# Narrow expert jobs of a mixture layer in plain float32, two 64-column stationary tiles side by side

## The chip, the core and the metric

One core of a Trainium2 chip. The metric is the device time of one execution in microseconds, the median of several runs. Engines: TensorE (PE, with its weight loads PEld), VectorE (DVE), ScalarE (ACT), GpSimd (POOL) and SyncE (SP), which here only issues DMAs.

## What is computed

A two-layer decoder step for 320 tokens (256 of a prompt, 8 x 8 of samples), width 1024. Layer 0 has a dense channel mixer, layer 1 a mixture of eight experts with the two best per token:

```python
def _swiglu(h, w_gate, w_up, w_down):
    return (jax.nn.silu(h @ w_gate) * (h @ w_up)) @ w_down

def _moe(h, w_router, b_router, w_gate, w_up, w_down):
    logits = (h @ w_router).astype(jnp.float32) + b_router.astype(jnp.float32)
    top_vals, top_idx = lax.top_k(logits, TOP_K)
    wts = jax.nn.softmax(top_vals, axis=-1)
    combine = jnp.sum(jax.nn.one_hot(top_idx, N_EXPERTS, dtype=jnp.float32) * wts[..., None], axis=-2)
    out = jnp.zeros_like(h)
    for e in range(N_EXPERTS):
        out = out + combine[..., e:e + 1] * _swiglu(h, w_gate[e], w_up[e], w_down[e])
    return out
```

w_gate and w_up are 1024 x 2816 per expert, w_down 2816 x 1024, all float32: 34.6 MB per expert.

## The kernel before

Everything up to 1207 us of the profile (both token mixers, the dense mixer, the router) is left as it is. Then the experts are worked off as jobs. A job takes up to 128 tokens (wide) or up to 64 (narrow) of one expert and streams all of that expert's weights. Jobs 0, 2, 4 and 6 are wide, jobs 1, 3, 5, 7 narrow; experts with more tokens get further narrow jobs at the end, up to six (`EXTRA`); with these inputs there is one, job 8. So nine jobs run, nine times 34.6 MB.

A job has 35 pairs of DMAs. Pairs 0 to 23 are gate and up columns in three column groups of eight pairs (one pair for each 128 rows of the 1024): 512 columns twice for gate and twice for up in groups 0 and 1 (1 MB per pair), 384 in group 2 (0.79 MB). Pairs 24 to 34 are two 128-row blocks of w_down each (1 MB). SyncE loads a pair n into slot n % 7 of the ring MRAW (L536) once pair n - 7 is used up (semaphore `m_used`). The first pair of a group is used up only with the second, since its second half of columns waits for a PSUM bank.

Weights are split into a rounded high part and a low part in the format fp32r, a matmul format that TensorE takes at one column per cycle: ScalarE copies a pair to MHI (`m_hi_part`, L1774, a ring of five), VectorE subtracts and writes MLO over the raw pair (`m_lo_part`, L1170). Both engines run ahead of TensorE by a fixed number of pairs in their program order, across the ends of jobs.

Wide job: tokens are split into XEH and XEL too, and each weight tile takes three matmuls (L2590 high x high, L2592 low x high, L2597 high x low; for w_down L2630, L2632, L2637 with the gated values GTH and GTL). Narrow job: the 64 tokens' high parts and their low parts stand side by side as 128 stationary columns, so two matmuls per weight tile (L2590, L2597; L2630, L2637) do it, and the two halves of the result are folded when it is turned: four PSUM tiles are copied by ScalarE (SG L1819, SU L1824), 88 small matmul calls pass them with FOLD (L2652) to the transposed layout, ScalarE and VectorE form silu(gate) x up and split it anew (L1849, L1414, L1807, L1368).

Between pairs, side work stands in a table by hand (`SIDE`): eight `combine` units in pairs 2 to 9 (L2549, L2550: the scaled output of the job before, YEH and YEL, through the placement matrix PTS into SA by VectorE L1409), six `turn` units (pairs 10, 11, 18, 19, 26, 27), `place` at 13, `pick` at 16, which frees POOL to gather the next job's tokens (L1989, 128 rows of 4 KB), and the two `fill` transposes at 28 and 30 that make the next job's stationary operand.

At a job's end ScalarE copies the output, scaled by the routing weight SW, to YEH (L1835) and VectorE makes YEL (L1390, `y_made`). TensorE's pair 1 of the next job waits for `y_made` before it takes the banks of the second column half. Each engine waits on its queue in order. After the last job SyncE loads three filler pairs (L562) that the ahead-running splits still count on. VectorE then releases the index semaphore for the gathers of the jobs that are not there (L1447), and POOL makes them one after another.

Pairs and landings below are counted per job from 0.

Of the kernel before, what the change touches and what calls it, by code (L numbers as in the profile page):

```python
# [99 lines left out]
TURN_OF = {tile_at(k)[0]: k for k in range(TURNS)}  # L100
TURN_PAIRS = {p: [k for _, what, k in units if what == "turn"] for p, units in SIDE.items()}
# [138 lines left out]
def build(nc, a, out):  # L240
    ctx = ExitStack()
    with ctx:
# [121 lines left out]
        SU = at("su", [P, 2, 512], F32, O_H1 + 18432)  # L364
        SGT = at("sgt", [P, 2, 4 * HALF], F32, O_H1 + 22528)
        FOLD = at("fold", [P, HALF], F32, O_H1 + 32768)
# [68 lines left out]
        half_lo = sem("half_lo")  # L435
# [36 lines left out]
        def _(sp):  # L472
# [80 lines left out]
            extra = sp.value_load(XI[0:1, 15:16], min_val=1, max_val=1 + EXTRA)  # L553
# [18 lines left out]
        def _(dve):  # L572
# [593 lines left out]
            def m_lo_part(job, n):  # L1166

                w = 4 * GROUPS[n % PAIRS // KD][1] if n % PAIRS < GPAIRS else 2 * D
                dve.wait_ge(m_hi, job * PAIRS + (n + 1))
                V.tensor_tensor(MLO[:, n % RAW_RING, 0:w], MRAW[:, n % RAW_RING, 0:w],  # L1170
                                MHI[:, n % HI_RING, 0:w].bitcast(F32), ALU.subtract).then_inc(m_lo, 1)
# [14 lines left out]
            def low_fill(k, number, half):  # L1186

                dve.wait_ge(xe_hi, number + 1)
                src, s = PS[:, FILL_BANKS[k], :].rearrange("p (k n) -> p k n", k=4), slice(4 * k, 4 * k + 4)
                if half:  # L1190
                    V.tensor_tensor(XEH[:, s, HALF:P], src[:, :, HALF:P], XEH[:, s, 0:HALF].bitcast(F32),
                                    ALU.subtract).then_inc(xe_out, 1)
                else:
                    V.tensor_tensor(XEL[:, s, :], src, XEH[:, s, :].bitcast(F32), ALU.subtract).then_inc(xe_out, 1)
# [56 lines left out]
            for k in range(2):  # L1251
                low_fill(k, k, False)
# [1476 lines left out]
```

## Time and profile before

| what | us |
|---|---|
| median of three runs (2090.72 to 2104.79) | 2097.79 |
| the profiled execution | 2101.74 |
| its span, first to last instruction | 2099.9 |
| TensorE busy, matmuls | 1964.0 |
| VectorE busy | 1427.4 |
| ScalarE busy | 1142.0 |
| mean granted clock of TensorE, share of 2.4 GHz | 0.977 |

The span is cut into stretches at the ends of jobs. A view of busy time by stretch gives for each engine the busy time and the number of instructions, then the granted clock, the DMA share and the rate. A timeline gives start, duration, engine, line, operation and tiles, and in brackets how long the engine sat idle before it and what released it. Matmuls are pipelined: the distance of two starts is what one costs, not its duration. A plain float32 matmul stands in the trace as two MATMUL instructions with two weight loads.

### The profile page before, as it was taken

To read this page: it belongs to the slowest core of one execution; us is meant where nothing else is said; L and a number is where in the kernel's file an instruction comes from. 1 tells how busy PE (TensorE), PEld (TensorE's weight loads), DVE (VectorE), ACT (ScalarE), POOL (GpSimd) and SP (SyncE) were. 2 spreads that over 40 slices of the span, in tenths; PEclk is the share of its full clock that TensorE was granted. 3 is DMA by queue.
4 is the path that set the end of the run, shared out by engine and by line. 5 is a ranking of instruction groups with operands and counts; after the bars stand their busy time and mean duration, and the time that the engine had idled before them with its cause. 6 is when DMAs were issued, how large, how long until landed. Compare 5 with 4: busy or idle time off the path is not lost. (4 is left out here: it accounts for less than half of the span.)

```text
span 2099.9 us, 34064 instructions
## 1 busy us (share of the span) xinstructions
PE 1964.0 (94%) x13043; PEld 1749.7 (83%) x13043; DVE 1427.4 (68%) x1617; ACT 1142.0 (54%) x1207; POOL 135.8 (6%) x172
## 2 busy tenths in 40 slices
PE   7999999999999999999999899989999988998894
PEld 5999999988999889989989788868777877887673
DVE  4476545555444455845455599998989898988985
ACT  4434334344443343423344477786778677777874
POOL 3100003200000030000140100000000000000000
PEclk8999999999999999999999999999999999999997
DMA  9635465564666454335565479999999999999995
GB/s 346 211 98 156 131 196 176 192 200 130 211 202 217 145 153 153 110 92 171 172 200 191 177 283 384 354 403 332 380 360 384 345 367 389 335 403 352 409 357 194
DMA packets 244412, 528.27 MB, mean 252 GB/s; under 512 B 18183, under 2 KB 142201, under 8 KB 244258
## 3 DMA queue, kind: packets, MB, share of 16 engines
q1 hardware_dynamic: 234304, 495.78, 66.2%
q0 software_dynamic: 9936, 30.34, 4.6%
q8 instruction: 105, 1.72, 0.3%
q14 instruction: 49, 0.40, 0.1%
q10 hardware_dynamic: 18, 0.04, 0.0%
HBM read 513.49 MB, written 12.59 MB: 251 GB/s over the span
## 5 line engine op out<-in xcount | busy, mean ns | idle before, releaser
L1170 DVE TENSOR_TENSOR mlo<-mraw,mhi 128x2048 fp32r<-128x2048 f32 (+1 forms) x317 | 680.2, 2167 | 24.3 <-ACT mhi L1774 22.4
L1774 ACT ACTIVATE mhi<-mraw 128x2048 fp32r<-128x2048 f32 (+1 forms) x318 | 576.9, 1822 | 205.2 <-DMA mraw<-in_w_exp_up 96.0
L584 DVE TENSOR_TENSOR wlo<-raw,whi 128x1024 fp32r<-128x1024 f32 x244 | 289.1, 1213 | 315.4 <-ACT whi L1483 314.3
L2092 PE MATMUL ps<-h1h,whi 128*128 128x320 f32 x1248 | 388.6, 323 | 6.6 <-DVE h1l L691 3.9
L2093 PE MATMUL ps<-h1l,whi 128*128 128x320 f32 x1248 | 373.6, 311 | 0.0
L1483 ACT ACTIVATE whi<-raw 128x1024 fp32r<-128x1024 f32 x244 | 247.7, 1046 | 116.7 <-PE ps L2477 44.8
L2590 PE MATMUL ps<-mhi,xeh 128*128 128x512 f32 (+1 forms) x864 | 281.1, 388 | 16.7 <-issue 6.7
L2092 PEld LDWEIGHTS ps<-h1h,whi 128*128 128x128 f32 x1248 | 237.8, 191 | 23.1 <-issue 17.8
L2093 PEld LDWEIGHTS ps<-h1l,whi 128*128 128x128 f32 x1248 | 237.9, 191 | 0.2 <-issue 0.2
L2597 PE MATMUL ps<-mlo,xeh 128*128 128x512 f32 (+1 forms) x864 | 230.3, 378 | 0.0
L2138 PE MATMUL ps<-h1h,wlo 128*128 128x320 f32 x1248 | 210.1, 311 | 0.0
L2590 PEld LDWEIGHTS ps<-mhi,xeh 128*128 128x128 f32 x864 | 160.6, 193 | 41.4 <-issue 9.9
L2138 PEld LDWEIGHTS ps<-h1h,wlo 128*128 128x128 f32 x1248 | 190.0, 189 | 0.4 <-issue 0.4
L2597 PEld LDWEIGHTS ps<-mlo,xeh 128*128 128x128 f32 x864 | 162.4, 192 | 25.5 <-DVE mlo L1170 0.9
L2592 PE MATMUL ps<-mhi,xel 128*128 128x512 f32 (+1 forms) x384 | 143.6, 374 | 0.0
L2630 PE MATMUL ps<-mhi,gth 128*128 128x512 f32 x396 | 131.5, 400 | 0.0
L2637 PE MATMUL ps<-mlo,gth 128*128 128x512 f32 x396 | 111.1, 402 | 20.8 <-DVE mlo L1170 20.3
L2637 PEld LDWEIGHTS ps<-mlo,gth 128*128 128x128 f32 x396 | 71.3, 188 | 50.1 <-DVE mlo L1170 36.7
L2630 PEld LDWEIGHTS ps<-mhi,gth 128*128 128x128 f32 x396 | 72.8, 188 | 13.8
L2592 PEld LDWEIGHTS ps<-mhi,xel 128*128 128x128 f32 x384 | 72.6, 189 | 8.8
L2092 PE MATMUL ps<-h2h,whi 128*128 128x320 f32 x256 | 77.0, 315 | 0.0
L1989 POOL DMA_INDIRECT xg<-h_rows,idx x15 | 18.1, 1204 | 897.0 <-DVE idx L1430 814.6
(445 smaller groups left out, 2792.1 us busy)
## 6 DMA issues: line engine op xcount, KB each, us to landing
mraw<-in_w_exp_down SPq DMA_DIRECT2D x198, 512.0 KB, 9.3
mraw<-in_w_exp_gate SPq DMA_DIRECT2D x150, 512.0 KB, 6.2
mraw<-in_w_exp_up SPq DMA_DIRECT2D x144, 512.0 KB, 7.6
raw<-in_w_in SPq DMA_DIRECT2D x128, 512.0 KB, 3.8
raw<-in_w_ada SPq DMA_DIRECT2D x64, 512.0 KB, 3.8
mraw<-in_w_exp_gate SPq DMA_DIRECT2D x72, 384.0 KB, 3.8
mraw<-in_w_exp_up SPq DMA_DIRECT2D x72, 384.0 KB, 5.0
pause<-in_w_ada SPq DMA_DIRECT2D x32, 512.0 KB, 7.2
```

The source lines that it names most:

```text
L584: V.tensor_tensor(WLO[:, u % RAW_UNITS, 0:w], RAW[:, u % RAW_UNITS, 0:w], WHI[:, h % HI_UNITS, 0:w].bitcast(F32), ALU.subtract).then_inc(l ...
L1170: V.tensor_tensor(MLO[:, n % RAW_RING, 0:w], MRAW[:, n % RAW_RING, 0:w], MHI[:, n % HI_RING, 0:w].bitcast(F32), ALU.subtract).then_inc(m_l ...
L1483: A.activation(WHI[:, h % HI_UNITS, 0:w], RAW[:, u % RAW_UNITS, 0:w], ACT.Copy).then_inc(hi_made, 1)
L1774: A.activation(MHI[:, n % HI_RING, 0:w], MRAW[:, n % RAW_RING, 0:w], ACT.Copy).then_inc(m_hi, 1)
L2092: M.matmul(out_, w, v[0], start=start, stop=False, skip_group_check=True)
L2093: M.matmul(out_, w, v[1], start=False, stop=False, skip_group_check=True)
L2138: ins = M.matmul(PS[:, 2 * j + m, 0:T], w[1][:, s], parts[0][:, k * T:(k + 1) * T], start=False, stop=(k == KD - 1), skip_group_check=True)
L2590: M.matmul(o_, XEH[:, k, :], hi_[:, s], start=(k == 0), stop=False)
L2592: M.matmul(o_, XEL[:, k, :], hi_[:, s], start=False, stop=False)
L2597: ins = M.matmul(PS[:, GROUP_BANKS[g][2 * i + j], 0:w], XEH[:, k, :], lo_[:, s], start=False, stop=(k == KD - 1))
L2630: M.matmul(PS[:, DOWN_BANKS[h], :], GTH[:, kf, :], hi_[:, s], start=(kf == 0), stop=False)
L2637: ins = M.matmul(PS[:, DOWN_BANKS[h], :], GTH[:, kf, :], lo_[:, s], start=False, stop=(kf == KF - 1))
```

## The change

Narrow jobs take the weights as they land. The 64 tokens are kept in plain float32 (XEF, GTF) as 64 stationary columns. Gate goes to PSUM rows 0 to 63 and up to rows 64 to 127 of the same bank, from two matmuls on two column halves of the array; the two 512-column halves of the down product likewise. ScalarE copies one PSUM tile in place of two per column half, the turn is 22 transposes in place of 88 calls with FOLD, and its result is not split. The semaphores of the splits count wide jobs alone. In a narrow job that precedes a wide one, ScalarE makes the next job's first three high parts in its steps 30 to 32 and VectorE the first two low parts after its last step. The output of a narrow job lies as 128 rows of 512 columns, so a combine after it reads rows 0 to 63 or 64 to 127. Job 7 is written out apart from the loop of extra jobs, and the three filler pairs are gone. Wide jobs keep their three matmuls.

```diff
+        XEF = at("xef", [P, KD, HALF], F32, O_H1 + 24576)
+        GTF = at("gtf", [P, KF, HALF], F32, O_I)
...
-            with sp.Fori(0, 1 + EXTRA) as k:
+            e = sp.value_load(XI[0:1, MAIN:NE], min_val=0, max_val=NE - 1)
+            load_job(MAIN, e)
+            extra = sp.value_load(XI[0:1, 15:16], min_val=0, max_val=EXTRA)
+            with sp.Fori(0, EXTRA) as k:
                 with sp.If(k < extra):
-                    e = sp.value_load(XI[0:1, bass.ds(k + MAIN, 1)], min_val=0, max_val=NE - 1)
-                    load_job(k + MAIN, e)
-
-            for n in range(HI_RING - 2):
-                sp.wait_ge(m_used, extra * PAIRS + (MAIN * PAIRS + n - RAW_RING + 1))
-                for j in range(2):
-                    sp.dma_start(MRAW[:, n, D * j:D * (j + 1)], wg[0, 0:P, 0:D]).then_inc(m_raw[n], 16)
...
+                    elif what == "turn" and split is None:
+                        f0, nf = tile_at(k)
+                        dve.wait_ge(gate_out, job * TURNS + (k + 1))
+                        V.tensor_tensor(GTF[:, f0:f0 + nf, :],
+                                        SGT[:, k % 2, 0:nf * HALF].rearrange("p (k n) -> p k n", k=nf),
+                                        PS[:, bank, 0:nf * P].rearrange("p (k n) -> p k n", k=nf)[:, :, HALF:P],
+                                        ALU.mult).then_inc(m_aux_out, 1)
...
+            def narrow_dve(job, split_next=None):
+
+                for p in range(PAIRS):
+                    if p == PAIRS - 1:
+                        dve.wait_ge(y_hi, job * 2 + 2)
+                        V.scalar_tensor_tensor(YEL[:, 0:512], PS[:, DOWN_BANKS[0], :], SW[:, 0:1],
+                                               YEH[:, 0:512].bitcast(F32), ALU.mult, ALU.subtract).then_inc(y_made, 1)
+                    if p == 0:
+                        next_weight(job)
+                    if split_next is not None and p - 1 in FILLS:
+                        low_fill(FILLS[p - 1], split_next)
+                    side_dve(job, p, None)
+                    if p == 14:
+                        choose(job + 1, split_next is None)
+                if split_next is not None:
+                    for n in range(2):
+                        m_lo_part(split_next, n)
+
+            wide_dve(0, 0, first=True)
             with dve.Fori(0, MAIN // 2) as two:
-                job_dve(two * 2 + 1, True, False, two)
-                job_dve(two * 2 + 2, False, True)
+                narrow_dve(two * 2 + 1, two + 1)
+                wide_dve(two * 2 + 2, two + 1)
+            narrow_dve(MAIN)
...
+                src = PS[:, FILL_BANKS[k], :].rearrange("p (k n) -> p k n", k=4)
+                if half:
+                    A.activation(XEF[:, 4 * k:4 * k + 4, :], src[:, :, 0:HALF], ACT.Copy).then_inc(xe_out, 1)
+                else:
+                    A.activation(XEH[:, 4 * k:4 * k + 4, :], src, ACT.Copy).then_inc(xe_hi, 1)
...
+            def narrow_act(job, half_next):
+                A.activation(SPARE[:, 0:1], ONES[:, 0:1], ACT.Silu)
+                for p in range(PAIRS):
+                    if p < GPAIRS and p % KD == KD - 1:
+                        g, w = p // KD, GROUPS[p // KD][1]
+                        for i in range(2):
+                            if i == 0:
+                                act.wait_ge(m_tile, job * 9 + (3 * g + 2))
+                            else:
+                                act.wait_ge(m_used, job * PAIRS + (p + 1))
+                            A.activation(SG[:, i, 0:w], PS[:, GROUP_BANKS[g][2 * i], 0:w], ACT.Copy).then_inc(prod_made, 1)
+                    if p == PAIRS - 1:
+                        act.wait_ge(m_used, job * PAIRS + PAIRS)
+                        A.activation(YEH[:, 0:512], PS[:, DOWN_BANKS[0], :], ACT.Copy, scale=SW[:, 0:1]).then_inc(y_hi, 2)
+                    if not half_next and 0 <= p + HI_RING - PAIRS < 3:
+                        m_hi_part(job + 1, p + HI_RING - PAIRS)
+                    for s, what, k in SIDE[p]:
+                        if what == "turn":
+                            nf = tile_at(k)[1]
+                            act.wait_ge(m_aux_in, job * JAUX + (s + 1))
+                            if k >= 2:
+                                act.wait_ge(m_aux_out, job * JAUX + (AHEAD + TURN_SLOT[k - 2] + 1))
+                            A.activation(SGT[:, k % 2, 0:nf * HALF].rearrange("p (k n) -> p k n", k=nf),
+                                         PS[:, 4 + s % 2, 0:nf * P].rearrange("p (k n) -> p k n", k=nf)[:, :, 0:HALF],
+                                         ACT.Silu).then_inc(gate_out, 1)
+                    if p in FILLS:
                         gathered(FILLS[p], job * 2 + (2 + FILLS[p]), half_next)
...
+            def combine(d, bank, half):
+
+                o_ = PS[:, bank, 0:T]
+                rows_ = slice(HALF * (d // 4), HALF * (d // 4) + HALF) if half else slice(0, P)
+                s = slice(d % 4 * P, (d % 4 + 1) * P) if half else slice(d * P, (d + 1) * P)
+                M.matmul(o_, YEH[rows_, s], PTS[rows_, :], start=True, stop=False)
+                return M.matmul(o_, YEL[rows_, s], PTS[rows_, :], start=False, stop=True)
...
+                    elif what == "turn":
+                        pe.wait_ge(prod_made, job * TURNS + (k + 1))
+                        for m in range(tile_at(k)[1]):
+                            ins = M.transpose(PS[:, bank, m * P:(m + 1) * P], SG[:, k % 2, m * P:(m + 1) * P], ident)
...
+            def narrow_pe(job, half_before):
+                pe.wait_ge(xe_out, job * 2 + 2)
+
+                def gate_up(p, halves):
+
+                    g, k, w = p // KD, p % KD, GROUPS[p // KD][1]
+                    for i in halves:
+                        for j in range(2):
+                            s = slice((2 * j + i) * w, (2 * j + i + 1) * w)
+                            ins = M.matmul(PS[HALF * j:HALF * j + HALF, GROUP_BANKS[g][2 * i], 0:w], XEF[:, k, :],
+                                           MRAW[:, p % RAW_RING, s], start=(k == 0), stop=(k == KD - 1),
+                                           skip_group_check=True)
+                            if k == KD - 1 and 2 * i + j < 3:
+                                ins.then_inc(m_tile, 1)
+                    return ins
+
+                for p in range(PAIRS):
+                    pe.wait_ge(m_raw[p % RAW_RING], job * (32 * (PAIRS // RAW_RING)) + 32 * (p // RAW_RING + 1))
+                    if p < GPAIRS:
+                        ins = gate_up_pair(job, p, gate_up)
+                    else:
+                        for kf in range(2 * (p - GPAIRS), 2 * (p - GPAIRS) + 2):
+                            if kf == 0:
+                                pe.wait_ge(prod_made, job * TURNS + 4)
+                            turned_in(job, kf)
+                            for h in range(2):
+                                s = slice((2 * (kf % 2) + h) * 512, (2 * (kf % 2) + h + 1) * 512)
+                                ins = M.matmul(PS[HALF * h:HALF * h + HALF, DOWN_BANKS[0], :], GTF[:, kf, :],
+                                               MRAW[:, p % RAW_RING, s], start=(kf == 0), stop=(kf == KF - 1),
+                                               skip_group_check=True)
+                    if ins is not None:
+                        ins.then_inc(m_used, 1)
+                    side_pe(job, p, half_before)
+
+            wide_pe(0, 0, False)
             with pe.Fori(0, MAIN // 2) as two:
-                job_pe(two * 2 + 1, True, two)
-                job_pe(two * 2 + 2, False)
+                narrow_pe(two * 2 + 1, False)
+                wide_pe(two * 2 + 2, two + 1, True)
+            narrow_pe(MAIN, False)
...
```

## Rows read from the trace of the kernel before

**Rows 1.** The page, its costliest group of instructions

```profile
L1170 DVE TENSOR_TENSOR mlo<-mraw,mhi 128x2048 fp32r<-128x2048 f32 (+1 forms) x317 | 680.2, 2167 | 24.3 <-ACT mhi L1774 22.4
```

**Rows 2.** Busy time by stretch: jobs 1 and 2, jobs 1 to 6, jobs 7 and 8, tail

```profile
core 0: us, PE busy (x) PEld busy (x) DVE busy (x) ACT busy (x) POOL busy (x), PEclk, DMA share, GB/s
1307.00:1396.30 89.30, 80.44 (x403) 66.58 (x401) 81.85 (x66) 70.87 (x63) 2.25 (x1) 0.96 0.99 377
1396.30:1497.10 100.80, 99.13 (x476) 84.76 (x475) 91.39 (x70) 72.83 (x54) 0.94 (x1) 0.98 0.95 359
...
1307.00:1880.60 573.60, 536.35 (x2629) 449.37 (x2628) 517.13 (x403) 432.21 (x348) 8.27 (x6) 0.99 0.97 368
1880.60:2062.50 181.90, 161.41 (x803) 132.17 (x803) 164.48 (x133) 143.72 (x128) 3.06 (x2) 0.97 0.99 377
2062.50:2099.90 37.40, 11.10 (x62) 9.36 (x60) 13.44 (x21) 9.68 (x19) 4.72 (x5) 0.66 0.33 109
```

**Rows 3.** Busy time by stretch: end of job 1, wide job 2, start of job 3

```profile
1375.00:1395.00 20.00, 18.70 (x95) 14.59 (x93) 18.50 (x13) 17.49 (x16) 0.00 (x0) 1.00 1.03 409
...
1405.56:1497.10 91.54, 91.54 (x451) 79.02 (x450) 82.13 (x64) 64.98 (x47) 0.94 (x1) 1.00 0.95 354
...
1501.00:1504.40 3.40, 3.40 (x10) 2.61 (x9) 3.40 (x3) 2.01 (x2) 0.00 (x0) 0.50 1.01 402
```

**Rows 4.** Timeline of ScalarE, job 1: start us, us, instruction, idle before it

```profile
1358.88 1.48 ACT L1774 ACTIVATE mhi<-mraw 128x1536 fp32r<-128x1536 f32 x1 [1.10 <-DMA mraw<-in_w_exp_up]
...
1363.39 1.92 ACT L1774 ACTIVATE mhi<-mraw 128x2048 fp32r<-128x2048 f32 x1 [2.75 <-DMA mraw<-in_w_exp_down]
...
1367.21 1.91 ACT L1774 ACTIVATE mhi<-mraw 128x2048 fp32r<-128x2048 f32 x1 [1.33 <-DMA mraw<-in_w_exp_down]
...
1399.71 1.25 ACT L1835 ACTIVATE yeh<-ps,sw 128x512 fp32r<-128x512 f32 x2
```

**Rows 5.** Timelines of VectorE and TensorE at the start of job 2

```profile
1400.42 1.41 DVE L1390 SCALAR_TENSOR_TENSOR yel<-ps,sw,yeh 128x512 fp32r<-128x512 f32 x2
...
1400.88 0.63 PE L2590 MATMUL ps<-mhi,xeh 128*128 128x512 f32 x1
1401.31 0.63 PE L2592 MATMUL ps<-mhi,xel 128*128 128x512 f32 x1
...
1405.56 0.39 PE L2590 MATMUL ps<-mhi,xeh 128*128 128x512 f32 x1
...
1407.37 1.07 PE L2597 MATMUL ps<-mlo,xeh 128*128 128x512 f32 x4
```

**Rows 6.** Plain float32 in tiles: TensorE's timeline, and one line's weight loads

```profile
301.47 1.34 PE L2138 MATMUL ps<-h2h,wlo 128*128 128x320 f32 x8
302.74 1.05 PE L2059 MATMUL ps<-raw,csf 128*9 128x256 f32 x16
303.72 0.41 PE L2092 MATMUL ps<-h1h,whi 128*128 128x320 f32 x1
...
828.67 1.15 PE L2263 MATMUL ps<-qq,kk 128*64 128x64 f32 x16 [0.49 <-DVE sc L856]
...
L2263 PEld LDWEIGHTS ps<-qq,kk x96: 132/138/138, 124.3 to 854.3; 128*64 128x64 f32 x96
```

**Rows 7.** Starts of jobs 7 and 3: timelines of ScalarE, TensorE and SyncE

```profile
1873.64 1.92 ACT L1774 ACTIVATE mhi<-mraw 128x2048 fp32r<-128x2048 f32 x1 [0.63 <-DMA mraw<-in_w_exp_up]
...
1880.87 0.62 PE L2590 MATMUL ps<-mhi,xeh 128*128 128x512 f32 x2
...
1500.31 0.72 PE L2590 MATMUL ps<-mhi,xeh 128*128 128x512 f32 x2 [2.81 <-issue]
...
1505.07 0.33 SPq L536 DMA_DIRECT2D mraw<-in_w_exp_gate  x1
```

**Rows 8.** The end: timelines of ScalarE and VectorE

```profile
2066.16 1.25 ACT L1835 ACTIVATE yeh<-ps,sw 128x512 fp32r<-128x512 f32 x2
...
2071.30 0.15 DVE L1447 COPY spare<-sw 128x1 f32<-128x1 f32 x1 [3.02 <-issue]
```

More of the change, by code:

```diff
@@ L99 @@
 TURNED = {tile_at(k)[0]: s for units in SIDE.values() for s, what, k in units if what == "turn"}
-TURN_OF = {tile_at(k)[0]: k for k in range(TURNS)}
-TURN_PAIRS = {p: [k for _, what, k in units if what == "turn"] for p, units in SIDE.items()}
+TURN_SLOT = {k: s for units in SIDE.values() for s, what, k in units if what == "turn"}
 PARTS = ["f", "q", "v", "i", "u", "g", "A", "ga", "gb", "B", "O"]
@@ L1184, in picked, with low_fill @@
                 V.tensor_copy(IDX[:, :], IW[:, 1:2]).then_inc(idx_made, 1)
[L1186 to L1194, printed above, removed]
+            def low_fill(k, split):
+                dve.wait_ge(xe_hi, split * 2 + (k + 1))
+                V.tensor_tensor(XEL[:, 4 * k:4 * k + 4, :], PS[:, FILL_BANKS[k], :].rearrange("p (k n) -> p k n", k=4),
+                                XEH[:, 4 * k:4 * k + 4, :].bitcast(F32), ALU.subtract).then_inc(xe_out, 1)
             for i in range(TT):
@@ L1375, in job_dve, with next_weight, wide_dve @@
+            def next_weight(job):
+                dve.wait_ge(sem("iw_made"), 1)
+                dve.wait_ge(y_made, job + 1)
+                V.tensor_copy(SW[:, :], IW[:, 0:1])
+            def wide_dve(job, split, first=False):
+                m_lo_part(split, 2)
+                m_lo_part(split, 3)
                 for p in range(PAIRS):
-                    if not half and p < GPAIRS and p % KD == KD - 1:
+                    if p < GPAIRS and p % KD == KD - 1:
                         w = GROUPS[p // KD][1]
@@ L2544, in pick @@
                 return ins
-            def combine(d, bank):
-                o_, s = PS[:, bank, 0:T], slice(d * P, (d + 1) * P)
-                M.matmul(o_, YEH[:, s], PTS[:, :], start=True, stop=False)
-                return M.matmul(o_, YEL[:, s], PTS[:, :], start=False, stop=True)
+            def combine(d, bank, half):
[4 more added lines that the diff above has]
+                return M.matmul(o_, YEL[rows_, s], PTS[rows_, :], start=False, stop=True)
             pe.wait_ge(p_made, 1)
@@ L2579, in lo_ready @@
                 def lo_ready(p):
-                    pe.wait_ge(m_lo, job * PAIRS + (p + 1))
+                    pe.wait_ge(m_lo, split * PAIRS + (p + 1))
                 def gate_up(p, halves):
@@ L2590, in gate_up @@
                             M.matmul(o_, XEH[:, k, :], hi_[:, s], start=(k == 0), stop=False)
-                            if not half:
-                                M.matmul(o_, XEL[:, k, :], hi_[:, s], start=False, stop=False)
+                            M.matmul(o_, XEL[:, k, :], hi_[:, s], start=False, stop=False)
                     lo_ready(p)
@@ L2630, in job_pe @@
                                 M.matmul(PS[:, DOWN_BANKS[h], :], GTH[:, kf, :], hi_[:, s], start=(kf == 0), stop=False)
-                                if not half:
-                                    M.matmul(PS[:, DOWN_BANKS[h], :], GTL[:, kf, :], hi_[:, s], start=False, stop=False)
+                                M.matmul(PS[:, DOWN_BANKS[h], :], GTL[:, kf, :], hi_[:, s], start=False, stop=False)
                         lo_ready(p)
```

267 lines of the change are left out of this document (103 added, 164 removed).

## The prediction

> **What bounds the kernel now.** I read the page first (its groups of instructions), then busy time by stretches cut at the jobs, then the timelines of TensorE, ScalarE, VectorE and SyncE around one boundary of each kind. The page's costliest group is the low split L1170, 317 times 2.17 us, 680 us in all [rows 1]; taken alone that would make VectorE the engine to relieve. By jobs [rows 2]: job 1 (narrow) takes 89.3 us, job 2 (wide) 100.8 us, the three narrow-plus-wide cycles together 573.6 us, the two last narrow jobs 181.9 us, the tail 37.4 us. These 755.5 us and the tail are all that the change can move; job 0 stays.
>
> A wide job is bound by TensorE: from pair 2 on it is busy for all of 91.54 us [rows 3], while the DMA share is 0.95. A narrow job is bound by the weights: at its end DMA moves 409 GB/s at a share of 1.03 [rows 3], so a full pair (1,048,576 bytes) comes every 2.56 us and a 384 pair (786,432) every 1.92. 27 x 2.56 + 8 x 1.92 = 84.5 us per job is the floor of the stream. The gather of the next tokens (512 KB) delays it near pair 24: 4.51 + 3.82 us where 5.12 would do (the splits at 1358.88, 1363.39 and 1367.21, each released by a landing, [rows 4]): 3.2 us more, of which 1.3 us is its bytes at 409 GB/s; I take 2.3. So a fully streaming narrow job is 86.8 us from last landing to last landing, 84.2 us from its first landing to its last.
>
> **What the change removes and puts in.** In a narrow job no raw pair is split: 35 low parts of 2.17 us in the mean leave VectorE [rows 1], 35 high parts of 1.5 to 1.9 us leave ScalarE [rows 4], and the ordered queues of these engines no longer tie TensorE to landings four pairs ahead. That is worth only what the stream allows.
>
> *TensorE, narrow.* Before, a pair is 8 matmuls of 512 columns at 0.226 us (eight from 1405.56 to 1407.37, [rows 5]); a wide pair has 12, 2.7 us. After, it is four plain float32 products, two side by side. The nearest row is L2059: float32, four column tiles at once. Its 16 instructions of 256 columns last from 302.74 to the next line's 303.72; less 0.10 for the change of mode that is 0.22 us per group of four [rows 6]. So one instruction streams 256 columns in 0.22 us whatever its neighbours do, and a product is two instructions. For 512 columns: 0.43 us each, a pair of tiles 0.86 us, two of them 1.72 us per pair, 1.29 us for 384 columns. Weight loads of 64 columns take 138 ns, but the 64-column float32 products of L2263 start 16 in 1.15 us [rows 6], one every 0.07, so loads overlap there. A job: 27 x 1.72 + 8 x 1.29 = 56.8, and for combines, turns, fills and picks 12 us, an estimate on the high side (the wide job's 91.5 us leave 6.8 beside 25 x 2.72 + 8 x 2.08 us of products in its last 33 pairs), 69 us in all, under the stream's 84. It is hidden, by the stream; if that cover goes it is rival A. Not shown anywhere: two tiles of 64 columns side by side. Bounds: 1.72 (full overlap) and 3.44 us (none); I take full overlap, since four tiles do it.
>
> *Start of a narrow job after a wide one.* At the wide end W the first narrow pair has landed 7.3 us ago (1873.64 against 1880.87, [rows 7]). From there the stream can run: last landing L = W - 7.3 + 84.2 = W + 76.9. After a loop jump TensorE starts 3.2 us late (1500.31 after an end at 1497.1, [rows 7]) and at half clock (0.50, [rows 3]). The ring's oldest slot is released only in pair 1; before, its refill was issued at 1505.07 [rows 7], 4.8 us after TensorE's start, and that much late for a stream that is to stay full: by the 5 us from an issue to its landing, 3 to 4 us are lost by pair 8. The new products of pair 0 and the first half of pair 1 (3 x 1.7 us at half clock) are about 1 us later. I add 4.5 us to job 3, 3 us to job 5, 1.5 us (a plain allowance) to job 1.
>
> *Start of a wide job after a narrow one.* This is what speaks against the change. ScalarE in `narrow_act` makes the next job's first three high parts at p = 30 to 32, ahead of the output copy at p = 34, as now (YEH starts at 1399.71, though TensorE ended 3 us earlier, [rows 4]). `narrow_dve` makes low parts 0 and 1 behind the output's YEL; now they are ahead of it. With L as zero: the next pairs land at 2.6, 5.1, 7.7; high part 2 is done at 9.7, YEH (one half, 0.65) at 10.4, YEL (0.7, half of the 1.41 in [rows 5]) at 11.2, low part 0 (a full pair, 2.3) at 13.6, low part 1 at 15.9. TensorE does four matmuls at 6 and idles till 13.6; the clock has then dropped, as it does now after the 3 us gap. At half clock a matmul comes every 0.43 us (1400.88, 1401.31, [rows 5]). Two low products (0.9), four of pair 1 (1.7), two more, six of pair 0 (2.6), six of pair 1 (1.4 to 2.6): regular work from L + 21.5, where now it starts 100.8 - 91.54 = 9.3 us after the narrow end, about L + 15.4. Every later instruction of TensorE queues behind this, and a wide job cannot catch up.
>
> *Combines in a wide job.* They now read rows 0 to 63 or 64 to 127, a row tile. A change of mode costs about 0.1 us in the row we have (L2138's eight take 1.34 us with the last one's own 0.31 in it, so one comes every 0.147 and the next was due at 302.65; L2059 starts at 302.74, [rows 6]). 8 x 2 x 0.095 = 1.5 us per wide job, three jobs: 4.6 us, uncovered.
>
> *A rule that speaks against the change.* In [rows 6] the 16 products of L2263 start every 0.06 to 0.07 us while each load lasts 0.138, so loads and products overlap. The Trainium skill, "TensorE: Matmul & The Clock Gate", section on packing small matmuls, says that a weight load overlaps a running matmul only where the row groups differ; here both tiles use all rows. By that rule a pair would be 2.8 us (rival A), by the row 1.72; the measurement is nearer to this case, and I go by it.
>
> *End.* The six filler loads go, and the last output copy no longer waits for the split of three of them. Before: TensorE ends at 2062.5 [rows 2], YEH starts only at 2066.16, VectorE's release of POOL is at 2071.30 [rows 8], and POOL's five leftover gathers, one after another, fill the 28.6 us to the end. After: TensorE's end + 0.7 + 0.7 + the same 3.0 us of skipped iterations = 4.7 us instead of 8.8. Saves 4.1. The gathers stay.
>
> **Sum**, against this execution's span. A cycle after: -7.3 + 84.2 + 21.5 + 91.5 = 189.9; three are 569.7, with the slips (4.5 + 3 + 1.5 = 9.0) and the combines (4.6) 583.3, against 573.6: +9.7. Jobs 7 and 8: -7.3 + 84.2 + 86.8 + 1.9 (the last pair's products) = 165.6 against 181.9: -16.3. Tail: -4.1. Together -10.7: span 2089.2. The profiled execution took 2101.74, 1.84 of it outside the span, so 2091.0; the median of the three runs, 2097.79, is 4 us lower than that execution: 2087.1.
>
> **Rivals**, as times of the median.
>
> A, slower: the two column tiles overlap only in part. If TensorE takes N per narrow job, the total is about 5N + 3 x (11 + 91.5 + 1.5) + 6.4 against 755.5 + 4.1, equal at N = 88, a pair of 2.3 us ((88 - 12)/33). At no overlap N = 33 x 3.44 + 12 = 125.5: +186 us, 2284. Loads of 64 columns that do not overlap (138 ns each, [rows 6]) make a pair 4 x 0.43 + 8 x 0.138 = 2.8 us, N = 104: 2176, with 0.02. That is what the rule of the Trainium skill above would give. A clock that stays at 1.2 GHz through the narrow jobs would cost the same as no overlap; against it, the clock holds 1.00 at the end of a narrow job now [rows 3], with 8 x 0.226 = 1.8 us of products in 2.56, as after. Partial overlap has 0.06, the clock 0.04; together 0.12.
>
> B, the start of the wide job is not lost: low parts come in time, regular work starts 11 us after the narrow end. Then the cycle is 8.6 us shorter: -26, 2061. For it: VectorE has little else to do then. Against: its order is written out, and the output copy it waits for stands behind three landings. 0.12.
>
> C, a narrow job streams no better than now (377 GB/s, [rows 2]) for a reason on the DMA's side: jobs 7 and 8 gain nothing, each cycle loses 6.1 (21.5 - 15.4) + 1.5, the tail gives 4.1: +19, 2117. Against: the last third of each narrow job runs at 409. 0.12.
>
> Forecast: 0.64; its own range 2074 to 2100.
>
> **Chances.** A measurement of this kernel can tell about 1% from no change, 21 us. Under 2077: B and a low part of the forecast (cheaper gather, 1 us x 5; no slips, 6; clock kept, 4): 0.30. Over 2119: A and a part of C: 0.18. Between: 0.52. The range runs from B to the near side of C, 2060 to 2110, and leaves out A and most of C.
>
> **What would show it.** Right: narrow windows at 409 GB/s and 79 to 80 us after a wide job, 87 for job 8; float32 products starting in twos, 0.43 us apart; wide windows of 109 to 111 us with 8 us of TensorE waiting for a low part at the start; VectorE's release 5 us after the last product. Wrong: narrow pairs over 2.3 us (A), wide windows near 101 (B), narrow windows near 90 with TensorE idle (C).

## The result and the profile after

| | before | after |
|---|---|---|
| median, us (6 runs each, side by side on one chip) | 2099.86 | 2082.22 (2075.73 to 2083.33) |
| span of the profiled execution | 2099.9 | 2079.5 |
| VectorE busy | 1427.4 | 1045.8 |
| ScalarE busy | 1142.0 | 805.0 |
| TensorE busy, matmuls | 1964.0 | 1933.5 |

The ratio of the runs is 0.9914, interval 0.989 to 0.9938: 18 us faster in the median, clear of the scatter. The forecast was 2087.1, 10.7 us less than before; the time lies within its range and in the middle one of its three cases, 2077 to 2119.

The page of the kernel after, two of its groups. The low split that led the page before with 317 times [rows 1] is down to the wide jobs' 140, and the plain float32 products of gate and up stand in its place, on TensorE:

```profile
L1165 DVE TENSOR_TENSOR mlo<-mraw,mhi 128x2048 fp32r<-128x2048 f32 (+1 forms) x140 | 298.9, 2164 | 10.9 <-ACT mhi L1778 10.4
L2686 PE MATMUL ps<-mraw,xef 128*64 128x512 f32 (+1 forms) x960 | 210.6, 567 | 16.4 <-DMA mraw<-in_w_exp_up 14.0
```

382 us less of VectorE and 337 us less of ScalarE give 20 us of span. Where these come from is in the busy time by stretch, cut at the ends of the jobs (columns as in [rows 2]): jobs 1 to 8 in order, the tail, and then jobs 1 to 6 and jobs 7 and 8 in one.

```profile
1305.30:1382.70 77.40, 71.46 (x337) 24.10 (x335) 10.02 (x25) 7.51 (x16) 0.94 (x1) 1.00 1.03 407
1382.70:1496.88 114.18, 105.02 (x478) 85.58 (x475) 86.84 (x65) 70.32 (x52) 0.95 (x1) 0.94 0.91 336
1496.88:1578.20 81.32, 72.28 (x337) 23.73 (x335) 10.02 (x25) 7.51 (x16) 0.94 (x1) 1.00 1.03 408
1578.20:1691.96 113.76, 104.60 (x478) 85.19 (x475) 86.67 (x65) 70.19 (x52) 0.94 (x1) 0.94 0.89 328
1691.96:1771.00 79.04, 71.68 (x337) 24.00 (x335) 10.02 (x25) 7.51 (x16) 0.94 (x1) 1.00 1.03 408
1771.00:1883.97 112.97, 103.35 (x479) 84.30 (x475) 86.56 (x65) 70.42 (x52) 0.94 (x1) 0.95 0.91 341
1883.97:1961.40 77.43, 71.42 (x335) 24.07 (x335) 9.32 (x24) 7.68 (x17) 0.94 (x1) 1.00 1.03 407
1961.40:2048.34 86.94, 73.34 (x339) 23.54 (x335) 8.67 (x23) 7.22 (x16) 0.95 (x1) 1.00 0.98 390
2048.34:2079.50 31.16, 9.79 (x64) 7.16 (x60) 8.87 (x17) 6.02 (x16) 4.72 (x5) 0.68 0.35 126
...
1305.30:1883.97 578.67, 528.39 (x2432) 326.91 (x2430) 290.13 (x270) 233.47 (x204) 5.66 (x6) 0.97 0.95 365
1883.97:2048.34 164.37, 144.76 (x672) 47.61 (x670) 17.99 (x47) 14.90 (x33) 1.89 (x2) 1.00 1.00 398
```

Job 1, narrow, went from 89.3 us at 377 GB/s [rows 2] to 77.4 at 407, and the wide job 2 after it from 100.8 to 114.2. So a cycle of the two gains nothing: 578.7 us for three against 573.6, +5.1. Jobs 7 and 8, narrow behind narrow, give 181.9 - 164.4 = 17.5; the tail gives 37.4 - 31.2 = 6.2; what stands before job 1 ends 1.7 earlier. Together -20.3, the difference of the spans but for rounding.

**The two tiles.** TensorE's timeline of job 1 (start, duration, line, x how many), with the combines of the job before between the pairs:

```profile
1311.98 1.94 PE L2686 MATMUL ps<-mraw,xef 128*64 128x512 f32 x8
1313.84 0.42 PE L2556 MATMUL ps<-pts,yeh 128*128 128x320 f32 x1
1314.10 0.31 PE L2557 MATMUL ps<-pts,yel 128*128 128x320 f32 x1
1314.33 1.94 PE L2686 MATMUL ps<-mraw,xef 128*64 128x512 f32 x8
```

Eight instructions of 512 columns (one pair of DMAs) take 1.94 us, the modelled end of the last included. In the single records they start in twos, 5 to 7 ns apart, and the next two mostly 0.429 us later; a pair costs 1.72 to 1.77 us.

**The start of a wide job.** Timelines of TensorE, ScalarE and VectorE around the start of job 2 (to be held against [rows 5]); the last narrow pair landed at 1381.3:

```profile
1387.15 0.79 PE L2640 MATMUL ps<-mhi,xeh 128*128 128x512 f32 x1 [3.85 <-DVE xel L1184]
...
1394.53 1.22 PE L2646 MATMUL ps<-mlo,xeh 128*128 128x512 f32 x2 [5.31 <-DVE mlo L1165]
...
1389.00 1.91 ACT L1778 ACTIVATE mhi<-mraw 128x2048 fp32r<-128x2048 f32 x1 [0.64 <-DMA mraw<-in_w_exp_up]
1390.82 0.67 ACT L1848 ACTIVATE yeh<-ps,sw 128x512 fp32r<-128x512 f32 x1
...
1391.52 0.75 DVE L1426 SCALAR_TENSOR_TENSOR yel<-ps,sw,yeh 128x512 fp32r<-128x512 f32 x1 [4.52 <-ACT yeh L1848]
1392.19 11.09 DVE L1165 TENSOR_TENSOR mlo<-mraw,mhi 128x2048 fp32r<-128x2048 f32 x5
```

Read it upwards from TensorE's second wait. The first low part starts at 1392.19, because VectorE makes YEL first (1391.52), which waits for YEH (1390.82), which stands on ScalarE behind a high part that waited for the landing of the third wide pair. The granted clock is 0.5 from 1386.9 to 1400.5: it fell at the end of the 3.85 us in which TensorE stood idle, and in that stretch the products come every 0.43 us.

### The profile page after: what moved, and what is told of

Read it like the earlier page. It is cut to its first block and busy times, and to the rows that moved or that the text cites. A ratio compares the mean times of both kernels' runs of the same rounds, so it can differ in the third digit from the quotient of the medians.

```text
span 2079.5 us, 32232 instructions
## 1 busy us (share of the span) xinstructions
PE 1933.5 (93%) x12713; PEld 1538.8 (74%) x12713; DVE 1045.8 (50%) x1392; ACT 805.0 (39%) x964; POOL 131.1 (6%) x172
## 5 line engine op out<-in xcount | busy, mean ns | idle before, releaser
L1778 ACT ACTIVATE mhi<-mraw 128x2048 fp32r<-128x2048 f32 (+1 forms) x140 | 253.4, 1819 | 171.2 <-DMA mraw<-in_w_exp_up 93.9
L1165 DVE TENSOR_TENSOR mlo<-mraw,mhi 128x2048 fp32r<-128x2048 f32 (+1 forms) x140 | 298.9, 2164 | 10.9 <-ACT mhi L1778 10.4
L2686 PE MATMUL ps<-mraw,xef 128*64 128x512 f32 (+1 forms) x960 | 210.6, 567 | 16.4 <-DMA mraw<-in_w_exp_up 14.0
L2640 PE MATMUL ps<-mhi,xeh 128*128 128x512 f32 (+1 forms) x384 | 151.9, 396 | 13.2 <-DVE xel L1184 11.6
L2686 PEld LDWEIGHTS ps<-mraw,xef 128*64 128x64 f32 x960 | 59.9, 136 | 120.4 <-issue 80.9
L2704 PE MATMUL ps<-mraw,gtf 128*64 128x512 f32 x440 | 106.5, 605 | 25.5 <-DMA mraw<-in_w_exp_down 24.4
L2646 PE MATMUL ps<-mlo,xeh 128*128 128x512 f32 (+1 forms) x384 | 103.3, 381 | 16.4 <-DVE mlo L1165 16.4
L2640 PEld LDWEIGHTS ps<-mhi,xeh 128*128 128x128 f32 x384 | 74.3, 194 | 30.3 <-issue 19.9
L2646 PEld LDWEIGHTS ps<-mlo,xeh 128*128 128x128 f32 x384 | 72.5, 193 | 29.3 <-DVE mlo L1165 18.5
L1358 DVE TENSOR_TENSOR sa<-sa,ps 128x320 f32<-128x320 f32 x72 | 34.9, 484 | 90.1 <-PE ps L2557 90.1
```

Source lines behind the costliest of these rows:

```text
L1778: A.activation(MHI[:, n % HI_RING, 0:w], MRAW[:, n % RAW_RING, 0:w], ACT.Copy).then_inc(m_hi, 1)
L2640: M.matmul(o_, XEH[:, k, :], hi_[:, s], start=(k == 0), stop=False)
L2646: ins = M.matmul(PS[:, GROUP_BANKS[g][2 * i + j], 0:w], XEH[:, k, :], lo_[:, s], start=False, stop=(k == KD - 1))
L2686: ins = M.matmul(PS[HALF * j:HALF * j + HALF, GROUP_BANKS[g][2 * i], 0:w], XEF[:, k, :], MRAW[:, p % RAW_RING, s], start=(k == 0), stop=(k ...
L2704: ins = M.matmul(PS[HALF * h:HALF * h + HALF, DOWN_BANKS[0], :], GTF[:, kf, :], MRAW[:, p % RAW_RING, s], start=(kf == 0), stop=(kf == KF ...
```

## The experiments

All are made from the kernel after. Times are medians, beside the kernel before on the same chip (2097.8 us for the first four, 2101.1 for the fifth to the seventh, 2096.2 for the eighth, 2096.0 for the last); for the gains I set them against 2082.2, the kernel after beside a kernel before of 2099.9, so a gain carries some us of difference between such groups. Experiments 1, 7 and 8 are single executions. In experiments 1, 2, 4 and 8 the output isn't the reference's, since products, columns or gathers are left out. The theory: a narrow job is bound by the stream of the weights, the two tiles are free, and the gain of the stream is given back at the start of each wide job, with a smaller part in the combines. The rivals: TensorE binds the narrow job, or the gather or the tail takes what is missing.

**1. Both tiles in the same half of the array.** Nothing can be side by side.

```diff
-  M.matmul(PS[HALF * j:HALF * j + HALF, GROUP_BANKS[g][2 * i], 0:w], XEF[:, k, :],
+  M.matmul(PS[0:HALF, GROUP_BANKS[g][2 * i], 0:w], XEF[:, k, :],
...
-  M.matmul(PS[HALF * h:HALF * h + HALF, DOWN_BANKS[0], :], GTF[:, kf, :],
+  M.matmul(PS[0:HALF, DOWN_BANKS[0], :], GTF[:, kf, :],
```

> Both stationary tiles of a narrow job use the same half of the array (up and the second down half are written over gate's rows, so the output is not the reference's). Same instructions, nothing side by side. Theory (two tiles overlap fully, 0.43 us per pair of passes): pairs of 512 columns go from 1.77 to 3.5 us, a narrow job takes about 125 us instead of 77 to 87, and with the start of the wide job 11 us after TensorE's end instead of 19 the whole is 190 to 210 us slower than the changed kernel, about 2280. Rival (they overlap only in part in the changed kernel): under 120 us slower.

Measured: 2280.75 us. TensorE's timeline, the same kind of pair as above, and the stretch of job 1:

```profile
1313.38 3.65 PE L2686 MATMUL ps<-mraw,xef 128*64 128x512 f32 x8
```

```profile
1302.13:1427.64 125.51, 125.51 (x336) 43.36 (x335) 10.70 (x26) 13.84 (x20) 0.94 (x1) 1.00 0.82 286
```

A pair takes 3.65 us where it took 1.94, and TensorE is busy for all of the 125.51 us. So in the kernel after the two tiles overlap completely; +198.5 us is what is lost without.

**2. Half of the columns of the narrow products.** The same instructions, each at half the length.

```diff
-  M.matmul(PS[HALF * j:HALF * j + HALF, GROUP_BANKS[g][2 * i], 0:w], XEF[:, k, :],
-           MRAW[:, p % RAW_RING, s], ...
+  M.matmul(PS[HALF * j:HALF * j + HALF, GROUP_BANKS[g][2 * i], 0:w // 2], XEF[:, k, :],
+           MRAW[:, p % RAW_RING, s.start:s.start + w // 2], ...
... (the products of w_down likewise, 256 columns of 512)
```

> Products of narrow jobs take only the first half of their columns (half of the result is left out); weights are loaded in full. Theory (narrow jobs are bound by the stream of weights): the same time within 3 us, 2079 to 2085 beside 2082 for the changed kernel, with narrow windows of 77 to 87 us at 408 GB/s. Rival (TensorE is on the path in narrow jobs, most of all at their start): 10 to 25 us faster.

Measured: 2082.19 us (2075.52 to 2083.9), the time of the kernel after. TensorE is busy for 52.0 us of job 1's 76.8, where it was 71.5 of 77.4, and the stream runs at 407 GB/s in both. So TensorE's products in narrow jobs are hidden behind the stream; what is saved in them brings nothing that these runs can show.

**3. The output copy ahead of the three high parts.** On ScalarE, at the end of a narrow job before a wide one:

```diff
-                    if not half_next and 0 <= p + HI_RING - PAIRS < 3:
-                        m_hi_part(job + 1, p + HI_RING - PAIRS)
+                    if not half_next and p == PAIRS - 1:
+                        for n in range(3):
+                            m_hi_part(job + 1, n)
```

> ScalarE copies the output of a narrow job before it makes the next wide job's first three high parts; nothing else changes. Theory (the wide job's start waits for the order of these queues: YEH behind three landings, YEL behind YEH, low parts behind YEL): low part 0 is ready about 7 us after the last landing instead of 13, regular work starts at L + 12.7 instead of L + 20, 7 us less in each of three wide jobs: 2058 to 2064. Rival (the start is held by landings or by the low clock): under 5 us in all, 2077 or more.

Measured: 2060.81 us (2058.49 to 2065.29), ratio to before 0.9824 (0.9778 to 0.9869). ScalarE, VectorE and TensorE at the start of job 2, and the stretches of wide jobs 2, 4 and 6:

```profile
1384.08 0.69 ACT L1848 ACTIVATE yeh<-ps,sw 128x512 fp32r<-128x512 f32 x1 [9.13 <-PE ps L2705]
...
1386.60 2.29 DVE L1165 TENSOR_TENSOR mlo<-mraw,mhi 128x2048 fp32r<-128x2048 f32 x1 [1.05 <-ACT mhi L1778]
...
1388.95 1.22 PE L2647 MATMUL ps<-mlo,xeh 128*128 128x512 f32 x2 [0.25 <-DVE mlo L1165]
```

```profile
1383.38:1490.51 107.13, 104.23 (x479) 84.90 (x475) 86.37 (x64) 69.97 (x51) 0.95 (x1) 0.97 0.95 358
1569.25:1677.27 108.02, 104.24 (x478) 84.97 (x475) 86.44 (x64) 69.96 (x51) 0.95 (x1) 0.97 0.94 352
1756.25:1862.97 106.72, 102.94 (x478) 84.06 (x475) 86.42 (x64) 69.86 (x51) 0.95 (x1) 0.98 0.95 362
```

TensorE's wait for the first low part is 0.25 us in place of 5.31, regular work (pair 2) starts 13.6 us after the last narrow landing in place of 20.7, and the wide jobs are 7.1, 5.7 and 6.3 us shorter. That is 19.0 of the 21.4 us; in the profiled execution job 3 is also 2.6 us shorter, since its stream starts earlier. One call that stands elsewhere gives back about half of the 39.5 us by which the three wide jobs had grown with the change. Half clock is part of it: 6.8 us at this start, 13.7 in the kernel after; the runs don't split the gain between the wait and the clock.

**4. Small loads in place of the gathers, from the third on.** It takes away 512 KB from each stream.

```diff
-  pool.indirect_dma_start(XG[:, :], None, HD, bass.IndirectOffsetOnAxis(IDX[:, 0:1], 0)).then_inc(xg_in, 16)
+  if job < 2:
+      pool.indirect_dma_start(XG[:, :], None, HD, bass.IndirectOffsetOnAxis(IDX[:, 0:1], 0)).then_inc(xg_in, 16)
+  else:
+      pool.dma_start(XG[0:1, 0:64], HD[0:1, 0:64]).then_inc(xg_in, 16)
```

> From the third on, the gather of 128 token rows is a 256-byte load (the tokens of later jobs are stale, their output wrong). Theory (a gather delays the stream by 2.3 to 3.5 us in each of five streaming narrow jobs, hidden in wide ones): 12 to 17 us faster from this, and about 12 more at the end, where five leftover gathers fill POOL's time: 2052 to 2060. Rival (a gather costs its bytes alone, 1.3 us each): 6 us and the end's 12, 2064.

Measured: 2055.2 us (2051.13 to 2058.62). Narrow jobs 1, 3, 5 and the tail:

```profile
1301.59:1377.69 76.10, 71.02 (x336) 24.29 (x335) 10.02 (x25) 7.53 (x16) 0.56 (x1) 1.00 1.03 407
1490.81:1567.87 77.06, 71.00 (x336) 24.22 (x335) 10.03 (x25) 7.53 (x16) 0.49 (x1) 1.00 1.03 408
1681.44:1758.56 77.12, 71.00 (x336) 24.25 (x335) 10.03 (x25) 7.53 (x16) 0.49 (x1) 1.00 1.03 408
2033.68:2052.90 19.22, 8.18 (x64) 5.96 (x60) 8.87 (x17) 6.02 (x16) 2.44 (x5) 0.89 0.20 69
```

First to last landing is 82.05, 82.86 and 83.01 us in jobs 1, 3 and 5, where it is 84.44, 84.89 and 84.87 with the gathers: one gather costs a narrow stream 1.9 to 2.4 us. Job 8 agrees (82.08 against 84.35). Job 7 doesn't: 85.14 us without a gather, from a first landing 9.9 us ahead of the wide job's end in place of 8.3; from that end to its last landing it is 75.3 us against 76.1. The tail is 11.9 us shorter.

**5. All 128 rows in the placement products of a narrow job's output.** A second placement matrix PTB holds rows 64 to 127 and zeros above, PTS is zeroed below; the sum is the same, and TensorE stays in one mode.

```diff
-                rows_ = slice(HALF * (d // 4), HALF * (d // 4) + HALF) if half else slice(0, P)
+                place = PTB if half and d >= 4 else PTS
...
-                M.matmul(o_, YEH[rows_, s], PTS[rows_, :], start=True, stop=False)
-                return M.matmul(o_, YEL[rows_, s], PTS[rows_, :], start=False, stop=True)
+                M.matmul(o_, YEH[:, s], place[:, :], start=True, stop=False)
+                return M.matmul(o_, YEL[:, s], place[:, :], start=False, stop=True)
```

> The placement matrix of a narrow job is kept twice, each with the other half's 64 rows zero, so that a combine reads all 128 rows and no product changes the row tiling in a wide job. Theory (each combine in the wide jobs 2, 4 and 6 costs 0.42 us more than with full rows, 3.35 us per wide job): 8 to 11 us faster than the changed kernel, 2071 to 2074, combine pairs back at 3.03 us. Rival (the extra 3.35 us come from elsewhere): no difference.

Measured: 2072.8 us (2070.29 to 2073.94), ratio 0.9862 (0.9846 to 0.9878): 9.4 less than the kernel after. A combine in wide job 2, first of the kernel after, then of this one:

```profile
1403.82 1.07 PE L2646 MATMUL ps<-mlo,xeh 128*128 128x512 f32 x4
1404.81 0.41 PE L2556 MATMUL ps<-pts,yeh 64*128 64x320 f32 x1
1405.07 0.30 PE L2557 MATMUL ps<-pts,yel 64*128 64x320 f32 x1
1405.30 0.50 PE L2640 MATMUL ps<-mhi,xeh 128*128 128x512 f32 x1
1405.64 0.40 PE L2641 MATMUL ps<-mhi,xel 128*128 128x512 f32 x1
```

```profile
1408.21 1.07 PE L2652 MATMUL ps<-mlo,xeh 128*128 128x512 f32 x4
1409.12 0.30 PE L2562 MATMUL ps<-pts,yeh 128*128 128x320 f32 x1
1409.26 0.31 PE L2563 MATMUL ps<-pts,yel 128*128 128x320 f32 x1
1409.41 0.40 PE L2646 MATMUL ps<-mhi,xeh 128*128 128x512 f32 x1
1409.64 0.40 PE L2647 MATMUL ps<-mhi,xel 128*128 128x512 f32 x1
```

From the start of the four low products to the second wide product after the combine it is 1.82 us against 1.43. The extra 0.4 us lies in four distances: 0.99 against 0.91, 0.26 against 0.14, 0.23 against 0.15, 0.34 against 0.23. A change of mode is paid before its first product and again before its second. Pair 2 to the end of the job is 91.54 us again, as before the change [rows 3], where the kernel after has 94.89.

**6. No gather for a job that isn't there.** GpSimd reads the number of extra jobs and makes a gather only for these; VectorE's release at the end goes.

```diff
-            for job in range(NE + EXTRA + 1):
-                if job > NE:
-                    pool.wait_ge(xg_in, 16 * job)
+            for job in range(NE + 1):
...
+            extra = pool.value_load(XI[0:1, 15:16], min_val=0, max_val=EXTRA)
+            for k in range(EXTRA):
+                with pool.If(extra > k):
+                    pool.wait_ge(idx_made, k + (NE + 2))
+                    pool.indirect_dma_start(...).then_inc(xg_in, 16)
```

> POOL gathers only for jobs that exist (a branch per extra job) and VectorE releases nothing at the end. Theory (the span ends with POOL's five leftover gathers, 26.6 us after the release; the output's own path ends about 8 us before them): 5 to 9 us faster than the changed kernel, 2073 to 2077. Rival (the output's path or the branches end as late): within 2 us.

Measured: 2069.96 us (2065.53 to 2070.97), ratio 0.9846 (0.983 to 0.9862), 12.3 less than the kernel after and more than I had expected. Its tail:

```profile
2049.33:2068.50 19.17, 8.17 (x64) 5.96 (x60) 8.86 (x17) 6.02 (x16) 0.00 (x0) 0.91 0.20 68
```

31.2 - 19.2 = 12.0, the whole gain: the chain of the last output alone is that much shorter than the chain of gathers, which I had put too near to it. It is the same tail as in experiment 4. Of that experiment's 27.0 us, 12 are thus the five leftover gathers, and 11 lie between the start of job 1 and the end of job 8 (732.1 us against 743.0), where the gathers in the narrow streams were; 3.7 us lie ahead of job 1 (1301.6 against 1305.3), where the kernels differ by one gather at most and executions differ anyway (1302.1 and 1305.7 in experiments 1 and 3).

**7. A longer loop body.** Each transpose of a narrow job's turns six times, 110 more products per narrow job, to bring back the break at the return of the loop (2.81 us of idle time before job 3, [rows 7]), which the kernel after doesn't have.

```diff
-                        for m in range(tile_at(k)[1]):
+                        for m in range(tile_at(k)[1] * (6 if again else 1)):
+                            m %= tile_at(k)[1]
```

> Each transpose of the turn in a narrow job is made six times over (110 products more per job, as many as half of what the fold calls were before), with the same result. Question: whether the loop's return gap of TensorE (3.2 us before the change, 0.3 after it) comes back with a longer loop body. Theory (gap set by the number of instructions in the loop body): gaps of 1 us or more at the starts of jobs 3 and 5. Rival (gap set by something else): 0.3 us as in the changed kernel. Time within 8 us of the changed kernel in either case.

Measured: 2097.37 us, 15 more than the kernel after and outside what was expected. The break is there, 2.75 us before job 3 and 2.59 before job 5, but it doesn't make the 15 us. Jobs 1, 3 and 5:

```profile
1305.67:1387.21 81.54, 81.19 (x446) 36.88 (x445) 10.01 (x25) 7.51 (x16) 0.94 (x1) 1.00 1.01 393
1500.81:1586.02 85.21, 82.85 (x447) 37.28 (x445) 10.02 (x25) 7.51 (x16) 0.95 (x1) 0.98 0.98 379
1699.60:1782.84 83.24, 81.04 (x446) 37.02 (x445) 10.02 (x25) 7.51 (x16) 0.94 (x1) 1.00 1.01 388
```

TensorE is now busy for 81.2 of job 1's 81.5 us: it has become the limit, and jobs 1, 3, 5 and 7 are 4 us longer each, also jobs 1 and 7, which have no loop return ahead of them and no break (0.3 us). The experiment mixed two causes, so the next one takes them apart.

**8. The longer body with half of the narrow columns.** Experiments 7 and 2 in one.

```diff
-                        for m in range(tile_at(k)[1]):
+                        for m in range(tile_at(k)[1] * (6 if again else 1)):
+                            m %= tile_at(k)[1]
...
-  M.matmul(PS[HALF * j:HALF * j + HALF, GROUP_BANKS[g][2 * i], 0:w], ...
+  M.matmul(PS[HALF * j:HALF * j + HALF, GROUP_BANKS[g][2 * i], 0:w // 2], ...
... (the products of w_down likewise)
```

> The transposes six times over in the turns of a narrow job, as in the kernel with the long body, but with half of the columns of the narrow products left out (the output is then partly not computed). The number of TensorE instructions in the loop is that of the long body, TensorE is no longer the limit of a narrow job. If the break of 2.6 to 2.8 us at the return of the loop comes with the number of instructions in the loop, it is there at the starts of jobs 3 and 5 here too. If it comes because TensorE runs without a pause up to the return, it is 0.3 us, as after the change. The time: about 2085 if narrow jobs are back at the stream (84 to 85 us between their first and last landings), with up to 5 more for the two breaks.

Measured: 2083.97 us. The first products of job 3, of the kernel after and of this one:

```profile
1497.20 1.94 PE L2686 MATMUL ps<-mraw,xef 128*64 128x512 f32 x8
```

```profile
1501.12 4.39 PE L2687 MATMUL ps<-mraw,xef 128*64 128x256 f32 x24 [2.44 <-issue]
```

Job 2 ends at 1498.29 here, so TensorE starts 2.8 us later, with the stream far ahead of it and without TensorE as the limit; in the kernel after it is 0.3 us (1496.88 to 1497.20), of which 0.23 is the last product itself. The break goes with the number of instructions in the loop: 920 products and 920 weight loads in one pass here, 810 of each after, 876 before. In the seven other kernels with 810 (experiments 1 to 6 and 9) it is 0.3 us too. Where there is a break, it stands only before jobs 3 and 5, where the loop returns. The Trainium skill, "Runtime: NRT & Kernel Launch", section on instruction fetch, says that TensorE's instruction memory holds 2048 instructions and that a taken branch to a target outside the window of pages held at the time has to wait for that page to be fetched. If the size of that memory decides, 1620 instructions (2 x 810) and 1752 (2 x 876) would lie on its two sides once the waits on semaphores, which aren't counted here, are added. That is a guess: no run shows the limit itself, or that the break is a fetch.

What the break costs is small here, and not settled in general. Job 3 takes 1579.36 - 1498.29 = 81.1 us with it and 81.3 without, but its first pair had landed 7.1 us ahead of the wide job's end and not 5.0, and its stream is 86.8 us from first to last landing against 84.9: 1.9 us may be the break's. Job 5 has a break of 2.8 us too, and its stream takes 84.7 us against 84.9. These are products of half the columns, with which TensorE catches up sooner after a break; with full ones and TensorE off the limit no run shows its cost.

**9. Experiments 3, 5 and 6 in one.**

```diff
+                    if not half_next and p == PAIRS - 1:
+                        for n in range(3):
+                            m_hi_part(job + 1, n)
...
+                M.matmul(o_, YEH[:, s], place[:, :], start=True, stop=False)
...
+                with pool.If(extra > k):
```

> The three edits with the right output together: YEH before the three high parts, all 128 rows in the products that place the rows of a narrow job, and no gather for an absent job. If the three gains lie in different places (the start of the three wide jobs, the 105 combines of the wide jobs, the narrow streams and the tail), they add: 21.4 + 9.4 + 12.3 = 43.1 us off 2082.2, about 2039 us. If the first two overlap (both shorten the wide jobs, and the stream of a wide job then has less slack) some of it is lost: up to 2048. If the high-parts edit takes the cover of the combine edit away altogether, about 2050.

Measured: 2041.63 us (2038.54 to 2044.21), ratio 0.9731 (0.9709 to 0.9754). Jobs 1 to 6, jobs 7 and 8, and the tail:

```profile
1302.11:1851.65 549.54, 516.55 (x2431) 327.55 (x2430) 293.75 (x276) 234.47 (x204) 5.67 (x6) 0.98 0.99 384
1851.65:2016.00 164.35, 146.03 (x671) 48.14 (x670) 19.82 (x51) 14.90 (x33) 1.89 (x2) 0.99 1.01 399
2016.00:2036.50 20.50, 10.47 (x64) 8.81 (x60) 8.86 (x17) 6.02 (x16) 0.00 (x0) 0.82 0.19 64
```

40.6 us of the 43.1 that the three gave alone; by the ratios to the kernel before it is 38 of 44. So they add, but for a few us that may be overlap or scatter. The cycles went from 578.7 to 549.5, 24.1 less than before the change. The DMA share over the cycles is 0.99 and the rate 384 GB/s, where the narrow jobs have 1.03 and 408: a stream that is full in wide jobs too would take at most 6% off the cycles, some 30 us (an estimate from these two rates).

## Why the prediction was right, and where it wasn't

Right, with the size:

- *The stream.* 84.2 us from first to last landing were forecast; five narrow jobs have 84.44, 84.89, 84.87, 84.35 and 84.35. The share of the gather, taken as 2.3 us, is 1.9 to 2.4 by experiment 4.
- *Jobs 7 and 8:* -16.3 forecast, -17.5 measured.
- *The tiles.* 0.43 us for two side by side, read off four tiles of another width, is 0.429. The formula for no overlap gave 2284; experiment 1 took 2280.75. The rule of the Trainium skill ("TensorE: Matmul & The Clock Gate", section on packing small matmuls) that a weight load overlaps a running matmul only where the row groups differ doesn't hold for these products (the estimate by it was 2176 us): two instructions start every 0.429 us, and the loads of both, 136 ns each in the mean, add nothing to that.
- *The loss at the start of a wide job,* its place and its order: last narrow landing to pair 2 forecast as 21.5, measured 20.7, 20.3 and 19.5. Experiment 3 shows that this order was the cause, and with it that what rival B describes, low parts in time, was one edit away. That the time agrees (2061 forecast, 2060.8 measured) is luck: B was 26 us under 2087.1, the edit gives 21.4 under 2082.2.

Wrong in size, with the right mechanism. By the profiled spans the change brought 20.4 us and not 10.7. Of the difference 4.6 us are the three cycles, 1.2 jobs 7 and 8, 2.1 the tail, and 1.7 stand before job 1, for which the sum had no term (job 1 begins anywhere from 1301.6 to 1308.3 in the kernels of the experiments, so this is scatter). The cycles came to 578.7 and not 583.3, by terms that partly cancel:

- *Slips, 9.0 us, the step that failed.* These are what a late start of TensorE was to take from the streams of jobs 1, 3 and 5. "After a loop jump TensorE starts 3.2 us late": this row of before was carried over, though the change shortens the loop, and the break goes with its length (experiments 7 and 8); after the change it is not there. From a wide job's end to the last narrow landing it is 76.0, 79.9 and 77.7 us for jobs 1, 3 and 5, forecast as 78.4, 81.4 and 79.9: 6.1 less in all, so that the slips came to 2.9. Whether the break would have cost the stream "3 to 4 us" stays open: in experiment 8, with lighter products, it is 1.9 and nothing. Job 3's 79.9 isn't a late start of TensorE but a first landing only 5.0 us ahead of the wide end where 7.3 was assumed. That belongs to this execution: in those of experiments 3, 5 and 6 this landing is 7.5, 7.1 and 6.7 us ahead, and the last one comes 77 to 78 us after the wide end. Why the stream fell back at the end of job 2 here (three landings 3.2 to 3.3 us apart) stays open.
- *Start of wide jobs:* 4.1 us less than 3 x 21.5.
- *Combines, 1.5 us per wide job.* The price 0.095 came from one change of mode, from its first product alone. A combine costs 0.42 us, 3.35 per wide job (94.89 against 91.54), 10 in all where 4.6 stood. Experiment 5 gives 9.4 back. The second start after a change was not looked at.
- *Tail, 4.1 forecast, 6.2 measured.* VectorE releases GpSimd 4.6 us after the last product (rows below), 8.8 before [rows 8], which is the 4.2. The other 2.0 is the five gathers, 25.7 us from the first to the end against 27.7; in the kernels of experiments 1, 2, 3, 5, 7 and 8, which end with the same five, it is 27.2, 25.9, 26.5, 27.5, 27.3 and 27.3, so much of this is scatter, and I name no cause.

VectorE's release, and GpSimd's first and last leftover gather after the change:

```profile
2052.90 0.15 DVE L1451 COPY spare<-sw 128x1 f32<-128x1 f32 x1 [2.39 <-issue]
...
2053.80 0.94 POOL L1994 DMA_INDIRECT xg<-h_rows,idx  x1 [46.78 <-DVE spare L1451]
...
2072.61 0.94 POOL L1994 DMA_INDIRECT xg<-h_rows,idx  x1 [3.37 <-DMA xg<-h_rows,idx]
```

Rival C is refuted by the windows at 407 to 408 GB/s, rival A by the pairs of 1.72 to 1.77 us and by experiment 1, which shows what no overlap would be.

## What to carry to other kernels

When work is taken off an engine, ask first what else waits in that engine's order: here 719 us less of ScalarE and VectorE brought 18, and moving one 0.7 us copy ahead of three waits for landings brought 21 more. Price an operation that the trace shows only once by the distance to the product after it as well, and a gap at a loop's return only after counting what the change does to the loop's length. Where a stage is bound by the stream, its products are free up to the stream's time and not an instruction further (experiment 2 against 7).

## What was not expected of the hardware

- Two float32 products of 64 stationary columns on the two column halves of the array run at the price of one: 0.429 us for each of the two instructions of a product, 512 columns at full clock, with weight loads of 136 ns beside them; on one half they take 3.65 us a pair against 1.94.
- A product on 64 rows between products on 128 costs about 0.1 us at each of four distances: both when the mode changes and one product later, on the way in and on the way out, 0.42 us in all (experiment 5).
- From the last product ahead of the return of TensorE's loop to the first behind it, it is 0.3 us with 810 products and 810 loads in the loop, 3.2 and 2.7 us with 876 (before jobs 3 and 5), and 2.6 to 2.8 us with 920.
- In experiment 2 the clock fell to 0.5 several times within a narrow job (0.942 in the mean of the span against 0.979), and the time stayed the same: there the slow clock cost nothing, since the stream bound the job.
